# Loading the second attention's first heads, and the first unit of branch weights, from inside the first attention's queue

## What is computed

```python
y_gqa = gqa_latent(q, k, v, k_ctx, v_ctx)                    # first attention, heads 0 to 7
y_na  = neighbourhood_latent(nq, nk, nv, nkc, nvc, rpb)      # second attention, heads 8 to 15, with a bias
y_fn  = fourier_mix(fu)
y_cv  = conformer_conv(cu, conv_w, conv_b, conv_g)           # 31 taps, normalised, silu
# merge: sum over branches i of  sigmoid(gate_i) * (y_i @ w_branch[i]),  then  @ w_out
```

## Time and profile before

| | |
|---|---|
| runs | 3122.49, 3120.59, 3122.03 us; median 3122.03 us |
| profiled execution | 3123.78 us, span 3122.0 us |
| PE busy | 2705.4 us, 87% |
| DVE busy | 1829.8 us, 59% |
| ACT busy | 1314.7 us, 42% |
| mean granted clock of PE | 0.937 of full speed |
| first attention, second attention | about 399 to 603 us, about 604 to 831 us |
| experts' stage | from about 1069 us |

### The profile page before, as it was taken

How to read it: one execution, slowest core, us unless ns; L and a number is a source line. 1 busy time by engine, 2 the same in 40 slices (tenths; PEclk the granted TensorE clock), 3 DMA queues, 4 the chain that set the end, 5 groups by cost and what they waited for, 6 DMA issues and landing times.

```text
span 3122.0 us, 32678 instructions
## 1 busy us (share of the span) xinstructions
PE 2705.4 (87%) x11871; PEld 2056.4 (66%) x11871; DVE 1829.8 (59%) x2802; ACT 1314.7 (42%) x1811; POOL 114.8 (4%) x172
## 2 busy tenths in 40 slices
PE   5689989788797499999569979999998997999998
PEld 1468566556576277777456756788887674678886
DVE  5642166576574688888654765544443676644444
ACT  5422256566422277777433235322233314532222
POOL 0022000000000100000100100000000000000000
PEclk9789999999999699999869989999998997999999
DMA  8478324443243399999712432223222244222222
GB/s 318 138 226 274 90 60 121 102 109 89 102 163 120 139 359 370 368 372 381 265 46 87 128 113 66 91 89 102 93 92 63 76 130 125 78 68 94 94 94 74
DMA packets 241578, 466.21 MB, mean 149 GB/s; under 512 B 67864, under 2 KB 90640, under 8 KB 241455
## 3 DMA queue, kind: packets, MB, share of 16 engines
q1 hardware_dynamic: 226383, 413.73, 40.2%
q0 software_dynamic: 15072, 50.87, 4.7%
HBM read 399.83 MB, written 64.72 MB: 149 GB/s over the span
## 4 chain that ended last, share of the span: by engine, by line
PE 61%; DVE 16%; ACT 9%; DMA 8%; issue 5%; POOL 1%; SPq 1%; DVEq 0%; ACTq 0%; POOLq 0%
PE BKP L772 40%; PE BKP L901 3%; PE BKP L944 3%; DMA G<-in_w_expert_gu_dram 3%; DMA W<-in_w_expert_gu_dram 2%; DVE WL L2550 2%; DVE hL L2550 1%; PE BKP L1007 1%; DVE WL L1894 1%; ACT WH L1693 1%; PE BKP L842 1%; PE SCP L877 1%; DVE WL L2048 1%; DVE G L2198 1%; PE SCP L1256 1%
## 5 line engine op out<-in xcount | busy, mean ns | idle before, releaser
L1894 DVE TENSOR_TENSOR WL<-W,WH 128x2048 fp32r<-128x2048 f32 x131 | 300.2, 2292 | 497.5 <-ACT WH L1321 495.9
L1321 ACT ACTIVATE WH<-W 128x2048 fp32r<-128x2048 f32 x131 | 250.6, 1914 | 648.4 <-PE BKP L772 555.2
L772 PE MATMUL BKP<-hH,WH 128*128 128x512 f32 x896 | 356.6, 398 | 15.9 <-DVE hL L2335 13.8
L772 PE MATMUL BKP<-hL,WH 128*128 128x512 f32 x896 | 351.8, 393 | 0.0
L772 PE MATMUL BKP<-hH,WL 128*128 128x512 f32 x896 | 351.8, 393 | 0.0
L772 PE MATMUL BKP<-WH,aH 128*128 128x512 f32 (+1 forms) x544 | 216.2, 397 | 22.4 <-DVE aL L2530 10.6
L772 PE MATMUL BKP<-WL,aH 128*128 128x512 f32 (+1 forms) x544 | 212.4, 390 | 0.0
L772 PE MATMUL BKP<-WH,aL 128*128 128x512 f32 (+1 forms) x544 | 212.2, 390 | 0.0
L772 PEld LDWEIGHTS BKP<-hH,WH 128*128 128x128 f32 x896 | 170.7, 190 | 56.9 <-issue 18.3
L772 PE MATMUL BKP<-WH,hH 128*128 128x512 f32 (+3 forms) x512 | 201.6, 394 | 6.9 <-ACT Z L1372 2.7
L772 PE MATMUL BKP<-WH,hL 128*128 128x512 f32 (+3 forms) x512 | 194.1, 379 | 0.0
(11 more groups left out here) (466 smaller groups left out, 5716.1 us busy)
## 6 DMA issues: line engine op xcount, KB each, us to landing
W<-in_w_expert_gu_dram SPq DMA_DIRECT2D x46, 1024.0 KB, 8.7
G<-in_w_expert_gu_dram SPq DMA_DIRECT2D x46, 1024.0 KB, 8.6
W<-in_w_in_dram SPq DMA_DIRECT2D x42, 1024.0 KB, 5.5
W<-in_w_up_dram SPq DMA_DIRECT2D x32, 1024.0 KB, 5.2
W<-in_w_down_dram SPq DMA_DIRECT2D x32, 1024.0 KB, 5.1
W<-in_w_expert_down_dram SPq DMA_DIRECT2D x24, 1024.0 KB, 7.9
G<-in_w_expert_down_dram SPq DMA_DIRECT2D x22, 1024.0 KB, 8.3
X<-in_w_in_dram SPq DMA_DIRECT2D x16, 1024.0 KB, 7.5
```

The source lines that it names most:

```text
L772: mm = pe.matmul(BK[j][:, 0:cols], lt, rh, start=start and a == 0, stop=stop and a == len(q) - 1, skip_group_check=True)
L1321: act.activation(WH[s][:], W[s][:], ACT.Copy).then_inc(sems["w_hi"], 1)
L1894: v.tensor_tensor(WL[s][:], W[s][:], WH[s][:].bitcast(F32), ALU.subtract).then_inc(sems["w_lo"], 1)
```

## The change

In SP's queue, `heads` for the first attention gets the second attention's bias loader. Instead of ending with the wait for both last outputs, it waits for the remainders of heads 6 and 7 one by one and loads queries and keys of heads 8 and 9, then their biases, then waits for the output copies of heads 6 and 7 one by one and loads the values of heads 8 and 9. The wait for the stored bias table moves ahead of the first attention. `heads` for the second attention skips its first part. Between the two calls SP loads the first unit of branch weights into `G[:, 4:8]`; the buffer's semaphore and the alternation are those of `W[s]`. ACT's rounding and DVE's remainder of that unit read `G[:, 4:8]`. The load of it after the second attention goes.

```diff
-            def heads(count, base, nk, bias=None, before=None, gates=None):
+            def heads(count, base, nk, bias=None, before=None, gates=None, first=True, next_bias=None):
...
-                for s in range(2):
-                    if before:
-                        before(s)
-                    qk(base + s, s)
-                for s in range(2):
-                    if bias is not None:
-                        bias(s, s)
-                    values(base + s, s)
+                if first:
+                    for s in range(2):
+                        if before:
+                            before(s)
+                        qk(base + s, s)
+                    for s in range(2):
+                        if bias is not None:
+                            bias(s, s)
+                        values(base + s, s)
                 T.skip("head_oe", 2)
...
-                T.skip("head_lo", 2)
                 T.skip("head_nm", 2 * NT)
-                sp.wait_ge(sems["head_oe"], T.next("head_oe", 2))
-                sp.sem_inc(sems["paused"], 1)
+                if next_bias is None:
+                    T.skip("head_lo", 2)
+                    sp.wait_ge(sems["head_oe"], T.next("head_oe", 2))
+                    sp.sem_inc(sems["paused"], 1)
+                else:
+                    for s in range(2):
+                        sp.wait_ge(sems["head_lo"], T.next("head_lo"))
+                        sp.sem_inc(sems["paused"], 1)
+                        qk(base + count + s, s)
+                    for s in range(2):
+                        next_bias(s, s)
+                    for s in range(2):
+                        sp.wait_ge(sems["head_oe"], T.next("head_oe"))
+                        sp.sem_inc(sems["paused"], 1)
+                        values(base + count + s, s)
...
-            heads(8, 0, KEYS, gates=3840)
             sp.wait_ge(sems["rpb_stored"], T.at("rpb_stored", 16 * 8))
...
-            heads(8, 8, KEYS, na_bias, gates=3840 + 2048)
+            heads(8, 0, KEYS, gates=3840, next_bias=na_bias)
+            load(G[:, 4:8, :], t["w_branch"][0, 0][:, 0:UN].rearrange("(k p) n -> p k n", p=P), f"w_landed{slot[0]}")
+            T.skip("w_lo")
+            slot[0] ^= 1
+            heads(8, 8, KEYS, na_bias, gates=3840 + 2048, first=False)
             load(MC[:, 0:656], t["k_moe"], "moe_landed")
...
-            unit(t["w_branch"][0, 0][:, 0:UN])
             unit(t["w_branch"][0, 0][:, UN:2 * UN])
...
-            def hi():
+            def hi(raw=None):
...
-                act.activation(WH[s][:], W[s][:], ACT.Copy).then_inc(sems["w_hi"], 1)
+                act.activation(WH[s][:], W[s][:] if raw is None else raw, ACT.Copy).then_inc(sems["w_hi"], 1)
...
             attend(8, lambda tt: KEYS, True, PTB_1, gates, True)
-            hi()
+            hi(G[:, 4:8, :])
...
-            def lo():
+            def lo(raw=None):
...
-                v.tensor_tensor(WL[s][:], W[s][:], WH[s][:].bitcast(F32), ALU.subtract).then_inc(sems["w_lo"], 1)
+                v.tensor_tensor(WL[s][:], W[s][:] if raw is None else raw, WH[s][:].bitcast(F32), ALU.subtract).then_inc(
+                    sems["w_lo"], 1)
...
             link(v.memset(ONE, 1.0))
-            lo()
+            lo(G[:, 4:8, :])
```

## The result

The changed kernel took 3107.23 us in the median of 5 runs (3102.86 to 3109.68), the kernel before 3122.49 us beside it (3120.59 to 3126.83). The ratio is 0.9947 with a 95% interval of 0.9934 to 0.9960, so it is faster by 12 to 21 us, clear of the 0.2% that I had set. The profiled execution took 3106.29 us with a span of 3104.5 us. PE's busy time is unchanged (2707.4 us before 2705.4), as it should be: the same work is done with less standing still.

What follows compares the result with a forecast made beforehand. The bound was load waits at the second attention's two ends, idling PE 10.12 and 13.84 us. Gains 6.7 + 8.1 = 14.8 us from the profiled 3123.78, less 1.75 to the runs' median, gave 3107.2 us; range 3102.5 to 3111.5.

Steps and rivals of the forecast that it cites:

- First boundary: Between first and second attention: early loads start PE 5.7 us sooner and the bias mask, with all behind it, 6.7 us.
- Second boundary: Between second attention and branch products: with weights already in G, PE restarts at 836.35 instead of 844.42, 8.1 us sooner.
- hidden at either end: Second branch-weight unit, landing at 837.8 or 843.22: ACT and DVE finish by 847.4 at latest, before PE wants it at 849.9.
- The clock: At PE's restarts: the new gaps of 4.4 and 5.8 us still leave PE at the lower level.
- rival (a): Clock holds through one or both shorter gaps: up to 4.0 us more gain, 3103.2 to 3106 us; chance 0.15.
- Low spells of the same length: After both gaps: PE's slow spell stays as long as before, twelve matmuls at 0.44 us each after the second.
- bound of 2.4 us: Second boundary: no fall of the clock at all would return 12 x 0.2 = 2.4 us.
- bound of 1.6 us: First boundary: no clock fall would return about 1.6 us, 0.5 from the first scores and 1.1 from seven more matmuls.
- seven more matmuls: Behind the first scores at the First boundary: without a clock fall these would return 1.1 us.
- The cover: Near 603.5 us: gate weights, head 9's values and the 1 MB load start together, costed at nothing.
- rival (c): Slower: moved loads delay attention one's gate stores, costing time from 26 us in flight; at 47 us, 3128; chance 0.02.
- Rival (b): Only half the change works, or a later stage takes part back; one boundary's gain lost gives 3113.9 or 3115.3; chance 0.10.

Runs made afterwards that it cites:

- again: The changed kernel unaltered, run and profiled once more on another chip; ratio to the kernel before 0.9952.
- first boundary alone: Changed kernel without the early branch-weight unit: only the loads of heads 8 and 9 move; median 3111.75 us, ratio to the kernel before 0.9974.
- unit rounded late: Changed kernel, but ACT rounds the early branch-weight unit only after the second attention's last output copy; one run, 3103.73 us.
- clock held: Changed kernel plus 36 PE transposes that compute nothing behind each attention's last value product; median 3099.43 us, ratio to the kernel before 0.9941.
- queries early: Changed kernel, but the four bias loads of heads 8 and 9 again wait for both output copies; ratio to the kernel before 0.9952.
- first branch ahead: Changed kernel, with first branch input's rounding and its and the unit's remainders made ahead of the second attention's last copy; ratio to the kernel before 0.9948.
- second boundary alone: Kernel before with only the first branch-weight unit loaded early, behind the second attention's first loads; median 3110.74 us, ratio 0.9978.
- biases early: Changed kernel, but the eight query and key loads of heads 8 and 9 wait for both output copies; median 3108.68 us, ratio to the kernel before 0.9974.
- both ahead: first branch ahead, plus head 8's rounding and remainders made ahead of the first attention's last copy; median 3092.96 us, ratio to the kernel before 0.9913.

## Why the prediction was right

The forecast, 3107.2 us, fell on the measured 3107.23 us. That it did so to a tenth is luck: single executions of the kernel before lie up to 21 us apart, and two misses inside the sum cancelled. By its steps:

**First boundary.** The starts of ACT (1.29 us behind the copy; 1.24 predicted) and PE (4.40; 4.3), and the mask (6.19; 6.0) are as worked out, and the kernel with this half alone shows the same. The gain was put at 6.7 us and measured 5.4. The step that was mis-sized is "Maximum, exponential and all that follows hang on that mask, so this boundary gives 6.7 us". The mask did gain 6.5, and the first two heads behind it as much; 1.1 us was then given back at ACT's waits for the gate product, 0.36 and 0.54 us at the two shown, where PE's clock was 0.91 instead of 1.00. The distance from the mask to the last copy, which "should stay" 215.1 us, was 216.27. The four other executions with the changed kernel's early loads and the same clock of 0.91 ahead of both waits (again, first boundary alone, unit rounded late, clock held) give back 1.0 to 1.2 us; the one with its biases late had 1.00 there and gives back 0.15. The issues themselves ended at 588.09, 3 us later than put, with 15 us to spare.

**Which load.** The prediction moved fourteen loads and gave them one price. The eight query and key loads carry about 5 of the 5.4 us; the biases alone had only 0.8 us left to give, nearly all of their wait being covered by the work that the queries start.

**Second boundary.** 8.1 us predicted, 7.9 measured, split into 6.4 for the transfer and 1.5 for the rounding. The second unit was bounded as hidden at either end. It was: ACT had to wait 2.37 us for it and DVE and PE nothing.

**The clock.** Both shorter gaps left the lower level, as taken, and rival (a) did not occur in the changed kernel. "Low spells of the same length" was wrong by one term: after the second gap the spell lasted six matmuls in place of twelve, which gave 1.1 us; in the other four with the same gap and no filler it gave 1.1 twice and 0.4 twice (ten low matmuls). The bound of 2.4 us for a second boundary without a fall was right: from 24.34 us before to 21.89 with the clock held is 2.45, of which the changed kernel has 1.1. The bound of 1.6 us for the first boundary was too high. Its 0.5 us for the first scores came (0.68 at the mask with the clock held, and 0.67 at head 8's output copy). Its 1.1 us for "seven more matmuls" are covered: six low gate products instead of three delayed no output copy, and with the biases alone early none of the twelve was low, PE's transposes came 2.7 us sooner than before, and head 8's copy only 1.3, like the mask (1.4). What the text had not counted is a lower clock in the middle of the attention, where ACT does wait for PE.

**The cover.** The gate stores landed in 2.3 to 7.2 us with a median of 3.0 (2.3 to 6.9 and 2.7 before). In the other kernels the median is 2.6 to 2.9 us and the longest 6.9 to 8.0, so these runs show no sure effect of rival (c)'s mechanism, and nothing near the 26 us in flight from which it would cost time. No wait for gate weights or for a query load appeared inside the second attention. Rival (b), half the change, is refused by the two halves.

**The sum.** 5.4 + 7.9 + 1.1 = 14.4 us beside 14.8, since what the first boundary lacked (1.3 us) the clock at the second nearly gave (1.1). The rest of the profiled difference, 3.1 us net, lies in stages with no changed instruction. The range was right, but one of its terms was not: I allowed 1 us of spread between executions on the strength of three runs that lay within 2 us.

## What to carry to other kernels

Where an in-order load queue waits for an output copy at the end of a phase, look which of the loads behind that wait need it: only the value buffers did here, and the small loads of the next phase's first operands could go 28 us sooner. Then ask the same of the compute engines, which gave another 9.5 us over the stretch: rounding and remainders for the next phase stood behind a copy of the last one that they did not read. When several loads move, price them one by one by what each releases; the one that starts the longest chain may carry nearly the whole gain. And to see where a gain goes, follow one repeated instruction through both traces: a delay of PE that no later copy shows costs nothing.

## What the runs showed that I had not expected

The kernel before spans 21 us over 35 runs on one chip (3107.39 to 3128.61), ten times the spread of its first three. Differences of 2 or 3 us between variants had to be read from stages of the trace: the stretch from the first copy to the convolution's sum repeats to 0.1 us between two profiles of the changed kernel, while the rest of the program varied by 10 us between the variants.

The granted clock differed in the middle of the second attention, far from any edited line, and decided how much of a gain arrived. At the first of the two ACT waits shown above, the eleven profiled executions fall into three groups by the clock of the 20 us ahead of it: 1.00 with 2.71 to 2.74 us of waiting (before, queries early, first branch ahead), 0.91 with 3.07 to 3.12 (changed, again, first boundary alone, unit rounded late, clock held), and 0.83 with 4.92 to 5.07 (second boundary alone, biases early, both ahead). Four heads later the last group, and first branch ahead, wait 1.6 us less than the others (2.02 to 2.07 us at 0.91, the others 3.65 to 3.72 at 0.83). What moved these low spells was not tried.

A gap of 4.44 us left PE at the lower level at its restart in five executions and not in the one with the first branch ahead, where the first score matmul still ran at the full clock (0.50 us) and the next one, 0.34 us later, already showed 0.56. Behind a gap of this length the level at the restart was not always the same.
